# Expert gates stored as running sums for heads 0 to 4, output passes of four and two tiles, residual loads spread

## What is computed

```python
q = (hn @ w_query).reshape(B, S, PEER_HEADS, 2, PEER_HALF)          # 8 heads
s = einsum('bshpd,hpkd->bshpk', q, sub_keys)                         # 2 x 128 scores a token and head
v1, i1 = top_k(s[..., 0, :], 16); v2, i2 = top_k(s[..., 1, :], 16)
cand = (v1[..., :, None] + v2[..., None, :]).reshape(..., 256)
cv, ci = top_k(cand, 16)
expert = i1[ci // 16] * 128 + i2[ci % 16]                            # of 16384 experts
gate = softmax(cv)
# per token, over the 8 x 16 chosen experts:
act = gelu(expert_u[expert] . x) * gate
h += sum(act * expert_v[expert]);   out = rmsnorm(h)
```

## Time and profile before

| | us |
|---|---|
| median of 3 runs | 3912.24 (3906.52 to 3913.24) |
| profiled execution | 3917.48 |
| its span | 3915.9 |
| TensorE busy in the span | 3655.3 (93%) |
| VectorE busy | 2659.9 (68%) |
| GpSimd busy | 1943.8 (50%) |
| ScalarE busy | 1241.5 (32%) |

### The profile page before, as it was taken

One profiled execution on the slowest core, in us unless ns is written; L12 is line 12 of the kernel. 1 busy time (PEld: TensorE's weight loads), 2 busy tenths in 40 slices (PEclk: granted clock), 3 DMA queues, 4 the chain that ended last, 5 costly groups with the idle time before them and its releaser, 6 DMA issues.

```text
span 3915.9 us, 55143 instructions
## 1 busy us (share of the span) xinstructions
PE 3655.3 (93%) x19324; PEld 3144.8 (80%) x19324; DVE 2659.9 (68%) x5202; ACT 1241.5 (32%) x1825; POOL 1943.8 (50%) x1352
## 2 busy tenths in 40 slices
PE   8989799998998999999999999999779999899998
PEld 6855498887876678899999999999558888787777
DVE  5443477775223348668887878877796666698887
ACT  3013343442112221333333333333233333333333
POOL 1023223231100118888888888888888888221120
PEclk9989899999999999999999999999899999999999
DMA  3249400002210135478888888887989998999997
GB/s 116 96 180 399 186 20 19 9 19 76 87 58 5 43 124 92 85 230 267 271 265 266 270 257 252 268 258 187 251 226 287 279 283 227 335 397 362 377 360 263
DMA packets 376223, 788.61 MB, mean 201 GB/s; under 512 B 136992, under 2 KB 245536, under 8 KB 342176
## 3 DMA queue, kind: packets, MB, share of 16 engines
q1 hardware_dynamic: 210208, 451.28, 34.2%
q0 software_dynamic: 165888, 336.01, 29.5%
HBM read 643.09 MB, written 144.05 MB: 201 GB/s over the span
## 4 chain that ended last, share of the span: by engine, by line
PE 25%; POOL 16%; DMA 7%; issue 6%; DVE 6%; DVEq 2%; ACT 1%; SPq 1%; POOLq 0%; ACTq 0%
POOL gates_d L2074 12%; PE peer_ps L2184 11%; PE peer_ps L2093 9%; PE peer_ps L2107 4%; DMA peer_gat<-gates_d 4%; DMA late_in<-gates_d 3%; POOL rows L2062 2%; POOL peer_rows L2062 2%; DVE late_rows L2467 1%; DVEq L2397 1%; DVEq L2481 1%; PE peer_ps L2130 1%; DVE peer_acc L2482 1%; DVE late_in L2489 1%; DVE peer_al L2501 1%
## 5 line engine op out<-in xcount | busy, mean ns | idle before, releaser
L2074 POOL DMA_INDIRECT gates_d<-peer_gates,peer_idx x768 | 1361.5, 1773 | 300.9 <-issue 220.9
L2093 PE MATMUL peer_ps<-high,peer_uh 128*128 128x384 f32 x2048 | 528.0, 338 | 39.3 <-DVE peer_ul L2384 33.4
L2093 PE MATMUL peer_ps<-low,peer_uh 128*128 128x384 f32 x2048 | 523.3, 336 | 0.0
L2093 PE MATMUL peer_ps<-high,peer_ul 128*128 128x384 f32 x2048 | 522.8, 336 | 0.0
L2093 PEld LDWEIGHTS peer_ps<-high,peer_uh 128*128 128x128 f32 x2048 | 369.3, 189 | 53.3 <-issue 46.3
L2184 PE MATMUL peer_ps<-peer_vh,peer_ah 128*128 128x512 f32 x1026 | 327.4, 401 | 52.8 <-DVE peer_al L2501 52.4
L2093 PEld LDWEIGHTS peer_ps<-low,peer_uh 128*128 128x128 f32 x2048 | 372.9, 189 | 0.0
L2093 PEld LDWEIGHTS peer_ps<-high,peer_ul 128*128 128x128 f32 x2048 | 372.7, 189 | 0.0
L2062 POOL DMA_INDIRECT late_rows<-in_expert_uv,peer_idx x108 | 135.4, 1253 | 416.5 <-DVE peer_acc L2482 367.4
L2184 PE MATMUL peer_ps<-peer_vh,peer_al 128*128 128x512 f32 x1026 | 320.0, 393 | 0.0
L2184 PE MATMUL peer_ps<-peer_vl,peer_ah 128*128 128x512 f32 x1026 | 318.9, 392 | 0.0
(11 more groups left out here) (478 smaller groups left out, 7588.4 us busy)
## 6 DMA issues: line engine op xcount, KB each, us to landing
late_in<-in_expert_uv SPq DMA_DIRECT2D x170, 512.0 KB, 5.5
gates_d<-mla_zeros POOLq DMA_DIRECT2D x128, 512.0 KB, 30.4
hidden_d<-peer_hid SPq DMA_DIRECT2D x128, 384.0 KB, 4.0
peer_raw<-in_expert_u SPq DMA_DIRECT2D x86, 512.0 KB, 5.1
peer_val<-in_expert_uv SPq DMA_DIRECT2D x86, 512.0 KB, 4.3
late_in<-hidden_d SPq DMA_DIRECT2D x170, 192.0 KB, 5.9
late_in<-gates_d SPq DMA_DIRECT2D x170, 192.0 KB, 6.9
first_raw<-in_expert_u SPq DMA_DIRECT2D x42, 512.0 KB
```

The source lines that it names most:

```text
L2074: pool.indirect_dma_start(gates_flat, bass.IndirectOffsetOnAxis(ap=idx[:, n, k:k + 1], axis=0), gates[:, n, k:k + 1], None, compute_op=ALU ...
L2093: last = nc.tensor.matmul(ps[i][:, a, 0:HD], w[:, cols], x[:, kc, a * HD:(a + 1) * HD], start=(kc == 0 and w is uh[i % 2] and x is high), ...
```

## The change

Three things. First, gates: for heads 0 to 4 (`WRITTEN = 5`) of the dense tiles the scatter writes (bypass) instead of adding. What it writes is the sum of the gate and of the gates of all earlier heads of the same token with the same expert; VectorE keeps experts and gates of heads 0 to 3 (`prior_e`, `prior_g`) and forms this in a new piece 6: compare 16 x 16h, multiply, reduce, add. Heads 5 to 7 add as before. Second, the passes are `((0, 1, 2, 3), (4, 5))`; with them `unit_order` has 32 dense units ahead of pass 0 instead of 24, the pieces are grouped otherwise and a unit takes five slots in the passes instead of three, 76 gathers instead of 28 lie in pass 0 (two rows every three slots) and 32 instead of 80 in pass 1 (two every seven slots); the 148 early ones are spread over units 7 to 33 instead of 7 to 29. Third, buffers and loads: expert_v loads go into the `raw` buffers, three block loads are issued before the hidden blocks end instead of one, and the residual is loaded at block 24 (2 MB) and block 80 (1 MB) of pass 0.

```diff
--- before.py
+++ after.py
...
 DENSE = NT - 2
-PASSES = ((0, 1, 2), (3, 4, 5))
-EARLY_SLOTS, PASS_SLOTS = 148, 28
+PASSES = ((0, 1, 2, 3), (4, 5))
+EARLY_SLOTS, PASS_SLOTS = 148, 76
...
 FIRST_UNIT = 3
+WRITTEN = 5
...
     for n in range(UNITS):
-        steps = ((0, 1, 2, 3, 4), (5,)) if slot < WT - 1 else ((0, 1), (2, 3), (4,), (5,))
+        if slot < WT - 1:
+            steps = ((0, 1, 2, 3, 4), (5, 6))
+        elif slot < WT + NK:
+            steps = ((0,), (1, 2, 3), (4,), (5, 6))
+        else:
+            steps = ((0,), (1,), (2,), (3,), (4,), (5, 6))
...
         sc, scw = [st.sb(f"sc{i}", [P, 2, NK]) for i in range(2)], st.sb("scw", [P, 2, NK])
-        cand, candw = st.sb("cand", [P, TOPK, TOPK]), st.sb("candw", [P, TOPK * TOPK])
-        sel = st.sb("sel", [P, 2, TOPK, TOPK])
+        work = st.sb("work", [P, 4 * TOPK * TOPK])
+        cand = work[:, 0:TOPK * TOPK].rearrange("p (a b) -> p a b", b=TOPK)
+        candw = work[:, TOPK * TOPK:2 * TOPK * TOPK]
+        sel = work[:, 2 * TOPK * TOPK:4 * TOPK * TOPK].rearrange("p (w a b) -> p w a b", w=2, b=TOPK)
...
                                              for i in range(HOME_ROWS, RING_IN)]
-        val = [st.sb("val", [P, D])] + [x[:, 0:D] for x in late_in]
-        act_in = [st.sb("act_in", [P, HALF])] + [x[:, D:D + HALF] for x in late_in]
-        gat = [st.sb("gat", [P, HALF])] + [x[:, D + HALF:2 * D] for x in late_in]
+            prior_e, prior_g = (home.enter_context(nc.sbuf_tensor(f"peer_{x}", [P, DENSE, WRITTEN - 1, TOPK], F32))
+                                for x in ("prior_e", "prior_g"))
+        val = raw
+        act_in = [st.sb(f"act_in{i}", [P, HALF]) for i in range(2)] + [hid[0][:, 0:HALF]]
+        gat = [st.sb(f"gat{i}", [P, HALF]) for i in range(2)] + [hid[0][:, HALF:T]]
...
         gates_flat = gates_d.rearrange("j i t -> (j i t)").unsqueeze(1)
-        done = [raw[0], raw[1], hid[0], hid[1]]
+        done = [x[:, a * D:a * D + D] for x in late_in for a in range(2)]
...
-            return {WT + NK - 1: 0}.get(b)
+            return {OUT - 2: 0, OUT - 1: 1}.get(b)
+
+        def earlier_heads(n):
+
+            head, tile = units[n]
+            return tile < DENSE and 0 < head < WRITTEN
...
             g -= EARLY_SLOTS // GROUP
-            return OUT + 13 + (g * 17) // 2 if g < PASS_SLOTS // GROUP else OUT + NK + 3 + 3 * (g - PASS_SLOTS // GROUP)
+            return OUT + 13 + 3 * g if g < PASS_SLOTS // GROUP else OUT + NK + 3 + 7 * (g - PASS_SLOTS // GROUP)
...
                 return 0
-            if i < 31:
-                return min(EARLY_SLOTS, EARLY_SLOTS * ((i - 7) * TOPK + k + 1) // (23 * TOPK))
-            return EARLY_SLOTS + (min(PASS_SLOTS, PASS_SLOTS * ((i - 32) * TOPK + k + 1) // (14 * TOPK)) if i > 31 else 0)
+            if i < 34:
+                return min(EARLY_SLOTS, EARLY_SLOTS * ((i - 7) * TOPK + k + 1) // (27 * TOPK))
+            return EARLY_SLOTS + (min(PASS_SLOTS, PASS_SLOTS * ((i - 35) * TOPK + k + 1) // (13 * TOPK)) if i > 34 else 0)
...
                     sp.wait_ge(row_used, EARLY_SLOTS)
-                if q == 1:
-                    sp.wait_ge(mm_done, WT + NK)
-                if q >= 3:
+                if q < 3:
+                    sp.wait_ge(u_low, OUT + q - 2)
+                else:
                     sp.wait_ge(split_done, q - 2)
+                if q == 2:
+                    sp.wait_ge(stored[0], 16 * (NK // 2))
...
                 sp.dma_start(gat[r][:, 0:n], gates_d[c][:, tokens]).then_inc(in_ready[r], 16)
+
+            def load_rest(p):
+                tiles = PASSES[p]
+                sp.wait_ge(h_stored, 16)
+                sp.dma_start(rest[p][:, :, 0:len(tiles) * P],
+                             h_d[:, :, tiles[0] * P:tiles[-1] * P + P].rearrange("k p t -> p k t")
+                             ).then_inc(rest_ready[p], 16)
...
                 sp.dma_start(hidden_d[c][:, 0:TD], hid[c % 2][:, 0:TD]).then_inc(stored[c % 2], 16)
-                if c == NK - 3:
-                    load_out(0)
-            load_out(1)
+                if c >= NK - 4 and c < NK - 1:
+                    load_out(c - (NK - 4))
             next_scores(OUT)
-            for p, tiles in enumerate(PASSES):
-                sp.wait_ge(h_stored, 16)
-                sp.dma_start(rest[p][:, :, 0:len(tiles) * P],
-                             h_d[:, :, tiles[0] * P:tiles[-1] * P + P].rearrange("k p t -> p k t")
-                             ).then_inc(rest_ready[p], 16)
...
             for q in range(2, 2 * NK):
-                load_out(q)
+                if q > 2:
+                    load_out(q)
                 next_scores(OUT + q - 1)
+                if q in (24, NK - 48):
+                    load_rest(0 if q == 24 else 1)
...
                     pool.indirect_dma_start(gates_flat, bass.IndirectOffsetOnAxis(ap=idx[:, n, k:k + 1], axis=0),
-                                            gates[:, n, k:k + 1], None, compute_op=ALU.add).then_inc(added[tile % 4], 16)
+                                            gates[:, n, k:k + 1], None,
+                                            compute_op=ALU.bypass if head < WRITTEN else ALU.add
+                                            ).then_inc(added[tile % 4], 16)
...
                 n = len(PASSES[q // NK]) * P
+                if q == 2:
+                    act.wait_ge(mm_done, OUT - 1)
...
                     halves()
-                highs_out(q)
+                if q > 1:
+                    highs_out(q)
...
                     dve.drain()
-                    tile = units[n][1]
-                    nc.vector.scalar_tensor_tensor(out=flat_e[:, :], in0=e12[:, 0, :], scalar=float(NK),
-                                                   in1=e12[:, 1, :], op0=ALU.mult, op1=ALU.add)
-                    nc.vector.tensor_scalar(gates[:, n, :], gexp[:, :], gsum[:, :], None, ALU.mult)
+                    head, tile = units[n]
+                    kept = tile < DENSE and head < WRITTEN - 1
+                    e = prior_e[:, tile, head, :] if kept else flat_e[:, :]
+                    nc.vector.scalar_tensor_tensor(out=e, in0=e12[:, 0, :], scalar=float(NK), in1=e12[:, 1, :],
+                                                   op0=ALU.mult, op1=ALU.add)
+                    last = nc.vector.tensor_scalar(gates[:, n, :], gexp[:, :], gsum[:, :], None, ALU.mult)
                     dve.drain()
+                    if kept:
+                        last = nc.vector.tensor_copy(prior_g[:, tile, head, :], gates[:, n, :])
                     if tile >= DENSE:
-                        nc.vector.tensor_copy(idx[:, n, :], flat_e[:, :]).then_inc(idx_ready, 1)
+                        last = nc.vector.tensor_copy(idx[:, n, :], e)
                     else:
-                        nc.vector.tensor_scalar(idx[:, n, :], flat_e[:, :], float(T), tok[:, tile:tile + 1], ALU.mult,
-                                                ALU.add).then_inc(idx_ready, 1)
+                        last = nc.vector.tensor_scalar(idx[:, n, :], e, float(T), tok[:, tile:tile + 1], ALU.mult,
+                                                       ALU.add)
+                    if not earlier_heads(n):
+                        last.then_inc(idx_ready, 1)
+                if piece == 6 and earlier_heads(n):
+                    head, tile = units[n]
+                    m = head * TOPK
+                    e = prior_e[:, tile, head, :] if head < WRITTEN - 1 else flat_e[:, :]
+                    same = work[:, 0:TOPK * m].rearrange("p (k j) -> p k j", j=m)
+                    nc.vector.tensor_tensor(same, e.unsqueeze(2).broadcast_to([P, TOPK, m]),
+                                            prior_e[:, tile, 0:head, :].rearrange("p h k -> p (h k)").unsqueeze(1)
+                                            .broadcast_to([P, TOPK, m]), ALU.is_equal)
+                    dve.drain()
+                    nc.vector.tensor_tensor(same, same,
+                                            prior_g[:, tile, 0:head, :].rearrange("p h k -> p (h k)").unsqueeze(1)
+                                            .broadcast_to([P, TOPK, m]), ALU.mult)
+                    dve.drain()
+                    nc.vector.tensor_reduce(e12[:, 0, :], same, AX.X, ALU.add)
+                    dve.drain()
+                    nc.vector.tensor_tensor(gates[:, n, :], gates[:, n, :], e12[:, 0, :], ALU.add).then_inc(idx_ready, 1)
...
                     others()
-                multiply(q_out)
-                lows_out(q_out)
+                if q_out > 1:
+                    multiply(q_out)
+                    lows_out(q_out)
```

## The result

The changed kernel takes **4149.89 us** (median of four runs, 4140.66 to 4159.58), the kernel before 3909.38 (four runs, 3906.15 to 3913.24): a ratio of 1.0615, 95% interval 1.0588 to 1.0642. The forecast was 3890, from 3852 to 3950. The profiled execution took 4148.83, its span is 4147.2 us, 231.3 longer than before.

A forecast was written before the change was run, and what follows sets the result against it. TensorE sets the floor; only its losses can shrink. Hidden blocks +21, start of pass 0 -38, turn -10, pass 1 +7, end -2: -22 us from 3917.5, runs' median 5.2 lower, so 3890 us, range 3852 to 3950.

The forecast's parts named there:

- A write costs 1.57 us with its issue: GpSimd's queue, hidden blocks: a write costs 1.27 + 0.30 us like a gather, where an add costs 2.10.
- Rival 1: Hidden blocks: a write costs GpSimd what an add costs, +134 us instead of +21, 4003 us in all; 15%.
- The scatters beside the query product: Ahead of the hidden blocks: no term and no cost forecast for the writes there.
- Unit 20 at 2133, then 574 us to gather 147: Hidden blocks: first adding unit (head 5) at 2123 plus 10 us, last early gather 574 us later at 2707, +21 us.
- Sums: Hidden blocks: piece 6 on VectorE exceeds its slack of 1.2 us in three slots and delays GpSimd's queue by 10 us.
- Start of pass 0: 2740 to 2950 us: five slots a unit cut TensorE's loss from 67 to 29 us, -38 us.
- The turn: Between the passes, 3300 to 3400 us: SyncE's wait on GpSimd's last scatters goes, 5 us lost remain, -10 us.
- End: After the last pass: one tile fewer to square and scale, -2 us.
- Pass 1: Second pass, two tiles: 398 GB/s asked, VectorE at 2.5 of 2.73 us a block, 30 us lost in 350, +7 us.
- rival 2: Second pass: a load's round through three buffers holds TensorE, 10.1 against 8.2 us, 80 us lost, 3940 us; 18%.
- The weighing of 358 against 396 GB/s: Second pass: the skill's limit of about 358 GB/s would give 375 us, 25 lost; the trace's 396 speaks against it.
- no wait at the first gate load: Sign at the change of passes: SyncE's queue doesn't wait at L1986; standing there would make the prediction wrong from the ground.

The follow-up runs named there:

- the run with late writes: The changed kernel with the first eight units of scatters, beside the query product, added instead of written, the other 28 written units left as writes: 4023.83 us.
- the two runs: The changed kernel with adds in all scatters, sums kept: 4057.57 us; the same with adds and without sums: 4048.62 us.

## Why the prediction was wrong

By its own steps:

- **A write costs 1.57 us with its issue**: right; 0.99 + 0.30 in the query product, 1.13 to 1.25 + 0.30 among the loads. Rival 1 (a write as dear as an add) is false. But its consequence, adds in all 34 units, was measured on the way: hidden blocks of 1248 us, +116 where it said +134.
- **The scatters beside the query product**: the failed step. The prediction priced a write only for GpSimd's own queue and began its sum at 1641. 115 writes lie ahead of the hidden blocks, and they cost 101.6 us. No rival was about this. The trace of before had no such write at all, so what a scatter that leaves every 1.3 us instead of every 1.9 does to the other engines was unknown there, and deserved a bound above nothing in each stage with scatters.
- **Unit 20 at 2133, then 574 us to gather 147**: the first add left at 2299. From there the model held: 2872.5 - 2299.3 = 573 us. Of the 166 us before, 102 are the late start and 64 came up beside the hidden blocks, where the prediction had TensorE lose nothing. In the run with late writes, whose hidden blocks start at 1610.4, the first add left at 2188.6, 56 late. TensorE had by 2197 done 2940 matmuls of the hidden blocks, 510 us of work at the price of the earlier trace rows, in 587: 77 lost, where the kernel before lost 20 in its first 513 us (2844 matmuls). That fits the gaps beside the writes, and the slow matmuls behind them, as the cause; no run takes these away and keeps the cheap writes. Behind gather 147 another 25 went, 79 us to the first pass matmul instead of 53: TensorE had 351 matmuls left instead of 298, and 11.4 us of gaps beside the 19 writes that follow. 21 + 64 + 25 = 110, measured 109.9.
- **Sums**: VectorE's 10 us can't be told apart from the gaps; with adds the two runs differ by 4 us of the hidden blocks (1252 against 1248) and 9 of the span, which is within what two runs of one kernel differ by. Its slack of 1.2 us in three slots should be 1.0 by its own row (12.4 us over 12 units); the term grows by 1 us.
- **Start of pass 0**, -38: -42.4. **The turn**, -10: -14.8. **End**, -2: -1.4. Right, mechanism and size.
- **Pass 1**, 30 lost: 99.6. The failed step is this term, which was taken from averages (398 GB/s asked of 396, VectorE at 2.5 of 2.73 us a block). The mechanism was rival 2's, which gave 80 lost at 18%, and its own condition was met: it decides from a landing of 5.3 us, and the loads that TensorE waited for in the changed kernel took some 9. With 0.85 of issue and 2.0 of splitting that is a round of 11.9 us against 8.2, 3.7 lost for each; measured are 3.1 to 5.1, and the slow matmuls behind them. What rival 2 had wrong is where a landing comes from: it scaled 8.4 us with the bytes of the load to 7.2 for every block, while the runs show about 4.9 without row work and 9 for the bunch that row sums hold back and two gathers precede.
- **Clock**: the prediction counted idle time alone. Each wait of some 3 us is followed by matmuls at half speed: 35 us of the 100 lost in pass 1.
- The weighing of 358 against 396 GB/s was settled for the trace: 399 GB/s for 400 us. The Trainium skill ("DMA: Bandwidth & Descriptors", Where 436 GB/s comes from) has 358 as the limit of a core. By that figure the stretch would have taken 446 us, an estimate; it took 400, so the page's limit did not hold here.

Of its list of signs, "writes near 1.3 us, adds near 1.8", "loss in the first 280 us of pass 0 under 30" and "no wait at the first gate load" came true, and the time was wrong by 260 us all the same: the signs tested the steps that were there, not the one that was missing. The sign for pass 1, near 380 us, did fail (449.5).

## What to carry to other kernels

When an instruction is swapped for a faster one, ask what its pace does to the engines that have nothing to do with it, and look at every stage in which it runs, not only at those where its own queue is the bound. For a ring of loads, write out the whole loop (issue, landing, each engine's turn for all buffers of the bunch, and whatever else stands in line on these engines and on the DMA engines), not the busy share; look at the few microseconds ahead of a wait, since a mean of 0.80 hid a stretch at 1.00; and price an idle time of TensorE with the slower matmuls behind it. Where a queue sets the pace, a cheaper item is worth having at just the place that needs no further work for it: 48 such writes took the ratio from 0.9989 to 0.9916, while 480 writes with their sums made the changed kernel 92 us longer than its twin with adds (4149.89 against 4057.57).

## What the runs showed of the hardware

- Indirect transfers of 128 indices, GpSimd's own time without crowding: write of 4 bytes 0.96 us, gather of 4 bytes or 8 KB 0.97 to 1.00, scatter with add 1.54, with 0.30 us between two.
- Writes of 4 bytes that leave every 1.26 us stop TensorE, its weight loads and VectorE again and again (TensorE 37.9 us in 23 waits and 37.8 in 32, the longest 2.9), with the DMA engines at 2% in two stretches of 5 us; adds, reads at the same pace, and writes 2.1 us apart do not. With gathers among them, some 10 writes in 20 us did it in one run and not in another. What is held up isn't shown: the gaps wait for nothing in the profile. One candidate is the supply of instructions, since unrelated engines stall at once. The Trainium skill ("Runtime: NRT & Kernel Launch", Instruction fetch mechanics) says that engines fetch through DMA queues of their own and that this is mostly hidden; no run here shows a fetch that was late.
- The granted clock falls to 0.50 while TensorE gets one matmul in about 2 us, and matmuls right after a wait of 3.38 us took 1.05 us for two instead of 0.61.
- A load loop three blocks deep idled TensorE with DMA engines at 0.80 and VectorE at 0.74 on average. Ahead of a wait the DMA engines stood at 1.00 for 6 us with VectorE idle: loads of 512 KB and less that left just behind two gathers of 1 MB landed in 8 to 9 us instead of 4.9.
